# Routing two mixture layers from the residual instead of from the normed activations

## The reference, cut to what matters

```
h      = x * rsqrt(mean(x*x) + EPS) * w * (1 + scale) + shift     # per channel w, scale, shift
scores = softmax(h @ router)                                      # 16 experts
for each expert: take the 2*tokens/16 tokens with the highest scores
expert(h[token]) = (silu(h[token] @ gate) * (h[token] @ up)) @ down, weighted by its score
x      = x + gate_vector * sum over experts
```

## Time and profile before

| what | value |
|---|---|
| runs, median (lowest to highest) | 2662.75 us (2660.42 to 2663.65) |
| the profiled execution: time, span | 2664.2 us, 2662.4 us |
| mean granted clock of PE | 0.971 |
| PE busy | 2478.3 us, 93% of the span |
| DVE busy, ACT busy | 1122.2 us, 753.8 us |
| PE loading weights | 1543.9 us |
| moved to and from HBM | 554.84 MB read, 13.11 MB written, 213 GB/s |
| layer 0 routing | 1217.6 to 1293.3 us |
| layer 1 routing and first expert | 2141.5 to 2213 us |

### The profile page before, as it was taken

The page is one execution under the profiler, slowest core; times in us unless marked ns, Lnnn a source line. Parts: engine busy times, 40 slices in busy tenths (PEclk is TensorE's granted clock), DMA queues, the critical chain, the costliest instruction groups (busy, mean ns, idle before and its releaser), DMA issues. The chain is left out here.

```text
span 2662.4 us, 39210 instructions
## 1 busy us (share of the span) xinstructions
PE 2478.3 (93%) x16700; PEld 1543.9 (58%) x16700; DVE 1122.2 (42%) x2162; ACT 753.8 (28%) x1546; POOL 50.7 (2%) x65
## 2 busy tenths in 40 slices
PE   8989999999899999988899999997999969988887
PEld 7856888888677778755433334344767743322222
DVE  5455633333787878776200000002566442111113
ACT  4345433333532223213111111112357521111002
POOL 0000000000000000000200000000000010000000
PEclk9989999999899999988999999998999979999999
DMA  5231322222210101026899999996230469999996
GB/s 204 107 142 78 131 85 104 96 102 86 78 50 32 50 32 50 32 111 237 320 387 395 379 393 382 397 376 256 98 159 2 190 253 360 428 428 428 428 427 279
DMA packets 58101, 570.47 MB, mean 214 GB/s; under 512 B 6815, under 2 KB 15015, under 8 KB 24776
## 3 DMA queue, kind: packets, MB, share of 16 engines
q1 hardware_dynamic: 50904, 544.37, 51.2%
q0 software_dynamic: 5584, 18.35, 2.3%
q10 hardware_dynamic: 1440, 5.24, 0.5%
HBM read 554.84 MB, written 13.11 MB: 213 GB/s over the span
## 5 line engine op out<-in xcount | busy, mean ns | idle before, releaser
L2922 PE MATMUL moe_gate<-ring,moe_xe_l 128*32 128x512 f32 (+1 forms) x1240 | 192.6, 599 | 15.1 <-DMA ring<-in_moe_gu 11.2
L3851 DVE SCALAR_TENSOR_TENSOR moe_hidden<-moe_hidden,moe_gate_rows,moe_up 128x512 f32<-128x512 f32 x31 | 23.2, 747 | 402.1 <-ACT moe_hidden L3774 402.1
L2922 PE MATMUL moe_up<-ring,moe_xe_l 128*32 128x512 f32 (+1 forms) x1240 | 190.0, 594 | 0.0
L3879 DVE SCALAR_TENSOR_TENSOR residual<-experts_psc,mod,residual 128x512 f32<-128x512 f32 (+1 forms) x78 | 54.8, 708 | 307.3 <-PE experts_psc L3715 169.9
L3635 PE MATMUL experts_py_l<-ring,experts_turn_l 128*32 128x512 f32 (+1 forms) x1136 | 144.8, 607 | 3.2 <-DMA ring<-in_moe_down 2.5
L1019 DVE TENSOR_TENSOR mlp_w_lo<-ring,mlp_w_hi 128x512 fp32r<-128x512 f32 x144 | 96.8, 689 | 97.7 <-ACT mlp_w_hi L964 97.4
L964 ACT CAST mlp_w_hi<-ring 128x512 fp32r<-128x512 f32 x144 | 86.5, 618 | 123.1 <-PE mlp_acc L920 123.1
L3774 ACT ACTIVATE moe_hidden<-moe_gate 128x512 f32<-128x512 f32 x31 | 18.5, 598 | 362.4 <-PE moe_up L2922 362.4
L2922 PEld LDWEIGHTS moe_up<-ring,moe_xe_l 128*32 128x32 f32 (+1 forms) x1240 | 49.6, 115 | 108.2 <-issue 108.2
L2922 PEld LDWEIGHTS moe_gate<-ring,moe_xe_l 128*32 128x32 f32 (+1 forms) x1240 | 44.9, 115 | 97.2 <-issue 68.3
L918 PE MATMUL mlp_acc<-mlp_h_hi,mlp_w_hi 128*128 128x512 f32 x256 | 100.0, 391 | 0.0
(11 more groups left out here) (645 smaller groups left out, 5106.9 us busy)
## 6 DMA issues: line engine op xcount, KB each, us to landing
ring<-in_moe_gu SPq DMA_DIRECT2D x91, 2048.0 KB, 11.0
ring<-in_moe_down SPq DMA_DIRECT2D x45, 2048.0 KB, 10.1
ring<-in_ada_w SPq DMA_DIRECT2D x24, 2048.0 KB, 7.8
ahead_wide_early<-in_moe_gu SPq DMA_DIRECT2D x9, 2048.0 KB, 30.5
ahead_wide_high<-in_moe_gu SPq DMA_DIRECT2D x9, 2048.0 KB, 30.4
ahead_wide_low<-in_moe_gu SPq DMA_DIRECT2D x9, 2048.0 KB, 30.5
normed<-in_moe_gu SPq DMA_DIRECT2D x9, 2048.0 KB, 30.5
ring<-in_w_up SPq DMA_DIRECT2D x8, 2048.0 KB, 7.5
```

The lines of the kernel that those rows point to most:

```text
L2922: last = core.nc.tensor.matmul(banks[m][at:at + n, :], xe_l[:, e, k, a:a + n], columns(2 * kk + m, FH * half, FH), start=(k == 0), stop=(k ...
```

## The change

The router product and the token rows take `core.x` in place of `core.h`; `core.h` is no longer made. The root, the gain and the shift are applied afterwards:

- DVE makes gain = w * (1 + scale) and multiplies the router by it once per stream (two small instructions). The router product starts when these are made. Its two streams now use different columns of one 32-column operand, and `fold` picks the stream's.
- PE sums shift against the unscaled router in 8 small products; ACT keeps the sum, and one product per stream spreads it. DVE multiplies the turned scores by the root and adds the spread sum.
- The copy of each turned half on ACT multiplies by the token's root.
- The copies after a gather apply gain and shift. These differ per channel block, so each copy of 4 blocks becomes 4 copies of one block (128x128), on ACT as well as on DVE.
- Two halves are turned ahead of the router product, and `keep_half(2)` stands ahead of the exponential on ACT.
- No modulation chunk is worked at the beginning. `late` is 2 in both layers: in layer 0 chunks 0 to 3 come after the token rows, 4 and 5 after `find`; in layer 1 both come after `find`. Their turns stand ahead of gather 0. In layer 1 `keep_columns` moves behind the gates.
- In layer 1 SP no longer waits for the token rows before it loads DEAD and ONCE.

```diff
-        late = 1 if ctx else 0
+        late = 2
...
-                    sp.wait_ge(tok_turned.handle, tok_turned.at(len(halves)))
                     wide.load(sp, WideRing.DEAD)
                     wide.load(sp, WideRing.ONCE)
...
-                        last = nc.tensor.transpose(bank[i % 4][:, k * P:(k + 1) * P], core.h[:, 4 * j + k, t * P:(t + 1) * P], core.ident[:])
+                        last = nc.tensor.transpose(bank[i % 4][:, k * P:(k + 1) * P], core.x[:, 4 * j + k, t * P:(t + 1) * P], core.ident[:])
...
-                scaling.spread_columns(pe)
-                for i in range(MOD_OPEN[layer]):
-                    part.step(pe, i)
+                turn_half(0)
+                turn_half(1)
                 pe.wait_ge(core.routers_loaded.handle, 32)
+                pe.wait_ge(routed.handle, routed.at(1))
                 for k in range(KD):
-                    pe.wait_ge(normed.handle, normed.at(k + 1))
...
+                for k in range(KD):
+                    last = nc.tensor.matmul(pa[0:32, 0:2], core.routers[:, k].rearrange("p l e -> p (l e)"), shift[:, k, :], start=(k == 0), stop=(k == KD - 1), tile_position=(0, 0))
+                last.then_inc(shift_summed.handle, 1)
...
+                pe.wait_ge(shift_kept.handle, shift_kept.at(1))
+                for i in range(len(streams)):
+                    last = nc.tensor.matmul(pl[:, (tiles + i) * E:(tiles + i + 1) * E], shift_col[:, i:i + 1].to_broadcast([2 * E, P]), core.ident[0:2 * E, layer * E:(layer + 1) * E], start=True, stop=True)
...
-                for i in range(MOD_OPEN[layer], part.n - late):
+                for i in range(part.n - late):
                     part.step(pe, i)
-                if late:
-                    part.turn(pe, part.n - 2)
+                if part.n > late:
+                    part.turn(pe, part.n - late - 1)
...
                     find("c", LT, tiles)
-                    part.products(pe, part.n - 1)
+                for i in range(part.n - late, part.n):
+                    part.products(pe, i)
...
-                    part.turn(pe, part.n - 1)
+                if not ctx:
+                    pe.wait_ge(gates_kept.handle, gates_kept.at(1))
+                for i in range(part.n - late, part.n):
+                    part.turn(pe, i)
...
-                    dst, src = keep(j, 0)
-                    nc.scalar.copy(dst, src).then_inc(kept[0].handle, 1)
+                    for q in range(4):
+                        dst, src, factor, offset = keep(j, 0, q)
+                        last = nc.scalar.activation(dst, src, ACT.Identity, bias=offset, scale=factor)
+                    last.then_inc(kept[0].handle, 1)
...
-                scaling.gains(dve)
-                for k in range(KD):
-                    scaling.scale(dve, k)
...
-                    dst, src = keep(j, 1)
-                    nc.vector.tensor_copy(dst, src).then_inc(kept[1].handle, 1)
+                    for q in range(4):
+                        dst, src, factor, offset = keep(j, 1, q)
+                        last = nc.vector.tensor_scalar(dst, src, factor, offset, ALU.mult, ALU.add)
+                    last.then_inc(kept[1].handle, 1)
```

More of the change, by code:

```diff
@@ L2954, in route_stage @@
         number = core.slot_number
-        fold = st.sb("fold", [P, E])
+        fold = st.sb("fold", [P, 2 * E])
+        gain = st.sb("gain", [P, len(streams), KD])
+        scaled_routers = st.sb("scaled_routers", [P, KD, 2, E])
+        shift_col = st.sb("shift_col", [2 * E, 2])
+        shift = core.mod[:, layer * 48 + 3 * KD:layer * 48 + 4 * KD, :]
+        rstd = core.norm_col[:, 2, 0:tiles]
         soft = st.sb("soft", [P, tiles, E])
@@ L3093, in _ @@
                 for t in range(tiles):
-                    last = nc.tensor.matmul(pl[:, t * E:(t + 1) * E], rows[:, t * P:(t + 1) * P], fold[:], start=True, stop=True)
+                    i = 0 if t < LT else 1
+                    nc.tensor.matmul(pl[:, t * E:(t + 1) * E], rows[:, t * P:(t + 1) * P], fold[:, i * E:(i + 1) * E], start=True, stop=True)
+                pe.wait_ge(shift_kept.handle, shift_kept.at(1))
+                for i in range(len(streams)):
+                    last = nc.tensor.matmul(pl[:, (tiles + i) * E:(tiles + i + 1) * E], shift_col[:, i:i + 1].to_broadcast([2 * E, P]), core.ident[0:2 * E, layer * E:(layer + 1) * E], start=True, stop=True)
                 last.then_inc(scores_turned.handle, 1)
@@ L3160, in keep_half @@
                     dst = tok[:, t] if t < LT else tok_ctx[:, t - LT]
-                    nc.scalar.copy(dst[:, j * 512:(j + 1) * 512], bank[i % 4][:]).then_inc(tok_kept.handle, 1)
+                    nc.scalar.activation(dst[:, j * 512:(j + 1) * 512], bank[i % 4][:], ACT.Copy, scale=rstd[:, t:t + 1]).then_inc(tok_kept.handle, 1)
                 def store(t):
@@ L3165, in store @@
                     act.dma_start(core.token_rows[t * P:(t + 1) * P, :], tok[:, t] if t < LT else tok_ctx[:, t - LT]).then_inc(tok_stored.handle, 16)
-                for k in range(KD):
[L3168 to L3173, removed]
                 nc.scalar.activation(warm[:], core.ones[0:1, :], ACT.Exp)
-                for i in range(1, MOD_OPEN[layer]):
-                    part.keep_row(act, i)
                 for i in range(2):
                     keep_half(i)
+                act.wait_ge(shift_summed.handle, shift_summed.at(1))
+                nc.scalar.copy(shift_col[:], pa[0:2 * E, 0:2]).then_inc(shift_kept.handle, 1)
+                keep_half(2)
                 act.wait_ge(shifted.handle, shifted.at(1))
                 nc.scalar.activation(soft[:], soft[:], ACT.Exp).then_inc(raised.handle, 1)
-                for i in range(2, 6):
+                for i in range(3, 6):
                     keep_half(i)
@@ L3192, in _ @@
                     store(t)
-                for i in range(MOD_OPEN[layer], part.n - late):
+                for i in range(part.n):
                     part.keep_row(act, i)
-                if ctx:
-                    part.keep_row(act, part.n - 1)
                 def keep_spread(i):
@@ L3230, in _ @@
                 link = Link(dve, chain)
-                scaling.gains(dve)
-                for k in range(KD):
-                    scaling.scale(dve, k)
-                nc.vector.tensor_reduce(fold[:], core.ident[:].rearrange("p (q w) -> p w q", w=32)[:, layer * E:(layer + 1) * E, :], AX_X, ALU.add).then_inc(folded.handle, 1)
+                for i, (c0, n, g, sc, sh) in enumerate(streams):
+                    nc.vector.scalar_tensor_tensor(out=gain[:, i, :], in0=sc, scalar=1.0, in1=g, op0=ALU.add, op1=ALU.mult).then_inc(gained.handle, 1)
+                dve.wait_ge(gained.handle, gained.at(len(streams)))
+                dve.wait_ge(core.routers_loaded.handle, 32)
+                for i in range(2):
+                    last = nc.vector.tensor_tensor(scaled_routers[:, :, i, :], core.routers[:, :, layer, :],
+                                                   gain[:, i % len(streams), :].unsqueeze(2).to_broadcast([P, KD, E]), ALU.mult)
+                last.then_inc(routed.handle, 1)
+                nc.vector.tensor_reduce(fold[:], core.ident[:].rearrange("p (q w) -> p w q", w=2 * E), AX_X, ALU.add).then_inc(folded.handle, 1)
                 dve.wait_ge(scored.handle, scored.at(1))
@@ L3283, in _ @@
                 last.then_inc(gates_kept.handle, 1)
+                if not ctx:
+                    part.keep_columns(dve)
                 if ctx:
```

32 lines of the change are left out of this document (17 added, 15 removed).

## The result

The changed kernel took 2678.00 us (median of 9 runs, 2671.51 to 2686.79) against 2663.65 us for the kernel before beside it: ratio 1.0053, 95% interval 1.004 to 1.0067. A second comparison of the same two kernels gave 2673.06 us against 2663.91, ratio 1.0031 (1.0022 to 1.004). The change makes the kernel 9 to 14 us slower by the medians. I had said 2667.5 us, 4.8 more than before, with 2674 as the upper end: the sign is right, the size is too small. The first comparison lies outside that range, the second just inside.

The account below looks back on a forecast made before the run. Both routing stages were taken as chains set by what waits last, the gathers deciding behind `find`. Layer 0 +2.3 and layer 1 +2.5 made +4.8 us on the median 2662.75: 2667.5 us, range 2655 to 2674.

Parts of the forecast that it names:

- Up to `find`: Both routing stages: scores 8.4 us sooner in layer 0 and 6.8 in layer 1, whose `find` ends 5.7 sooner.
- Chunk 3 ahead of the positions: Layer 0: PE waits for modulation chunk 3, landing in 9.7 us, so of 6.9 us gained only 3.8 stay.
- Layer 0, gathers: Layer 0 behind `find`: gu 1 and gu 2 loading beside the gathers cost +5.1 us, keeps in four +1.0.
- Layer 1, gathers: Layer 1 behind F, the end of `find`: loads slow the gathers, PE waits for each pair; +8.2 us.
- PE's own late products: Layer 1: modulation products behind `find` cost PE about 2.5 us ahead of gather 0, less what a full clock returns.
- The keeps in layer 1: Layer 1's copies after a gather, four in place of one: no cost was entered for them.
- Rival 1: Gathers keep their pace beside ring loads in both layers: -6 to -9 us, about 2655; chance 0.24.
- Rival 2: Queues share more evenly in layer 1: together about 0, 2662.7 us; chance 0.16.
- Rival 3: Layer 1: PE waits inside the first expert, its clock falls over three chunks; 8.4 us more, 2676; chance 0.14.

Follow-up runs that it names:

- hold: Changed kernel with layer 0's loads of gu 1 and gu 2 issued only once the last gathers have landed; median 8 to 13 us below the changed kernel.
- before_hold: Kernel before the change, with layer 0's load of gu 2 issued only once the last gathers have landed; 4.2 us faster by the median.
- after_again: The changed kernel, unchanged, profiled once more; layer 1's fourth chunk came at `find` + 38.6 us, against + 40.7 in the first profile.
- before_late2: Kernel before the change, with only two modulation products moved behind `find` in each layer (late = 2); 16 us slower than the kernel before (2664.37 us).
- hold_layer1: Changed kernel with layer 1's loads of gu 1, gu 2 and all behind them on SP issued only once the last gathers have landed; 2677.73 us.
- late_l1: Changed kernel with no modulation product behind `find` in layer 1 (late = 0 there), layer 0 as changed; 9 to 14 us faster by the medians.
- one_keep: Changed kernel with late = 1 in layer 0, 0 in layer 1, and one plain copy per gathered half; 3.3 us faster than with four.

## Why the prediction was wrong in size

**Up to `find`: right.** Scores 9.0 us sooner for 8.4 in layer 0, 7.9 for 6.8 in layer 1 (there the granted clock was 1.00 in place of the mean that I took, and the product took 1.92 us). The shift product took 0.64 us, all of it beside the score copy or nearly so; the additions were 1.3 for 1.5. Layer 1's `find` came 5.8 us sooner for 5.7.

**Chunk 3 ahead of the positions: right in kind, 1 us off.** Its load took 11.6 us to land, not 9.7 (issued at 1236.7, PE waited until 1248.37). Of 8.8 us by which DVE was sooner 2.8 stayed, where I had 3.8 of 6.9.

**Layer 0, gathers: right in kind, 1 us short.** I had +5.1 and +1.0; measured +7.3 from `find` to the experts, and +6.7 in the second execution. hold takes back 7.8 us of that span with two loads away, before_hold 3.7 with its one load away. By these, one profile each, the load more cost about 4.1 us, less than my 5.1, and the other 3.2 us are the keeps and PE's late product, for which I had 1.0. The queues showed 0.30 to 0.39 MB of gathered rows in 4 us in three stretches, 75 to 98 GB/s, for the 126 that I read from the earlier trace rows. Nor do those rows show equal turns, as I wrote: 158 packets stand against 57, so with equal turns the ring load had no packet waiting for part of that time. The stretches with 99 against 99 and 97 against 95 show them.

**Layer 1, gathers: the step that failed.** I wrote that PE "waits for each pair, and turns the last group at F + 36.6", +8.2. In the profile of the scored result, whose time is the median of its nine, the term measured +12.3. Two things were wrong. The rate: 126 GB/s was read beside a single ring load; with loads queued one behind the other it was 75 to 85 from F + 8 to F + 16 and at most 170 up to F + 24, so that groups 2 and 3 landed at F + 24 and not at F + 18. And what decides: not the last pair. All gathered bytes had moved by F + 32, sooner than my F + 34.5. It was the first late pair, because behind it PE has a chain of its own: from 2207.78 to 2224.45, 16.7 us for turns and two chunks, without another wait for rows. F + 24 + 16.7 is the 40.7. I had added PE's work to the last landing only.

The other executions of this code do not repeat that pattern. In after_again PE did wait for each pair and turned the last one from F + 36.6 on, as forecast; the term was +10.2, with the long wait for ACT in it. In hold PE waited for none, and it was +7.1. So the term lies between 7 and 12 us around my 8.2, and the first late pair decided in only one of three executions of this code (before_late2, with the same two late products, has the pattern too: one wait of 3.12 us, for groups 2 and 3).

**PE's own late products: under-estimated.** I gave them 2.5 us "less what a full clock returns"; hold_layer1 shows 5.9 at the low clock. In the changed kernel's first profile gather 0 was turned 2.1 us later than in late_l1, and the wait of 6.07 us behind it hid that. In hold_layer1 they kept the cure of the loads from working.

**The keeps in layer 1: put at nothing.** In late_l1, with no late product, the fourth chunk came 29.3 us behind `find` for 28.4 before; one_keep takes back 1.3.

**Rivals.** Rival 1, gathers keep their pace, is excluded by 85 GB/s beside the loads against 368 alone, and for layer 0 by hold. Rival 2, an even share, by the fifth of the bytes that the gathers had. Rival 3's mechanism is seen once, not three times: the chunk behind the 6.07 us wait took 5.5 us (2209.68 to 2215.20), the next one, at the full clock, 3.6, so 2 us of the 12.3. Its total, 2676, was nearest to the result, for mostly another reason.

**The rest.** By stages the change costs 10.8 us in the first profile (forecast 4.8) and 7.6 in the second. Layer 0 is 2 us above its forecast in both, layer 1 3.9 us in the first and 0.8 in the second. What is beyond the stages in the first, 3 us, lies in unchanged code. The two comparisons, +14 and +9 us by their medians, have intervals that only touch, at 1.004; no run tells why.

## What to carry to other kernels

When work is moved behind a point, list the transfers that it frees as well as its instructions: two modulation products looked free on PE, and the loads that they released starved the gathers behind them. In these runs small-packet gathers beside large-packet loads got an equal number of packets while both queues had some waiting, hence a fifth of the bytes. Holding the load until the last gather has landed paid in layer 0 (7.6 and 3.4 us) and not in layer 1, where PE's own late work was as long and the held load came late. When transfers of a series are late, add the consumer's remaining work behind the first late one, not only behind the last; and after each cure ask what is late next (here PE's late products, then the keeps, then the token row stores). And read one stage in more than one execution before naming the wait that decides it.

## What was not expected of the hardware

Gathers alone moved 1.47 MB in 4 us (368 GB/s), beside queued ring loads 0.34 MB (85 GB/s) while those took 1.36: together 425 GB/s, of which the gathers had a fifth. The same two late products of layer 1 took 3.20 and 1.92 us in one execution, where the granted clock rose from 0.50 to 1.00 during the first, and 3.64 and 3.64 in another, where it stayed at 0.50, with the same instructions on PE; a cost read on PE from one execution can be off by nearly a factor of two. And a chunk of 2 MB that lands in 7.8 us at the median took 11.6 to 15.5 us beside token row stores and its neighbours.
